# Seventh-products for the V columns, quarter products in the recurrence, and one block for experts and combination

## The reference

```python
# first block: attention with forget gates, then an MLP with squared ReLU
mod = silu(c) @ w_ada + b_ada                 # six vectors: shift, scale, gate, twice
h = rms_norm(x, norm_mix) * (1 + sc_m) + sh_m
qkv, f = h @ fox_w_in                         # 3 x 1024 columns, and 16 for the gates
x = x + g_m * (attention(norm(q), norm(k), v, cumsum(log_sigmoid(f))) @ fox_w_out)
x = x + g_f * (square(relu(h2 @ w_mlp_in)) @ w_mlp_out)

# second block: pooling and a recurrence per head (64 wide), then routed experts
z = x @ w_in ; zm = z + (z_prev - z) * mu     # z_prev: the token before
r, k, v = zm columns ; w, a, g from small two-step products
state = state * decay + sa * (kk * a) + v * k ; out = state . r   # token by token
y = (group_norm(out) + bonus) * g
h = layer_norm(alpha * x + [pool, y] @ w_out)
y = sum of 2 of 32 experts: (silu(h @ gate) * (h @ up)) @ down, weighted
out = layer_norm(alpha * h + y)
```

## Time and profile before

| what | value |
|---|---|
| median of three runs | 3013.24 us |
| profiled execution, its own time | 3023.13 us |
| its span | 3021.4 us |
| PE busy | 2836.5 us (94%), 18832 records |
| DVE busy | 1538.4 us (51%) |
| ACT busy | 725.1 us (24%) |
| POOL busy | 265.6 us (9%) |

### The profile page before, as it was taken

How to read it: one execution, slowest core, us unless ns; L and a number is a source line. 1 busy time by engine, 2 the same in 40 slices (tenths; PEclk the granted TensorE clock), 3 DMA queues, 4 the chain that set the end, 5 groups by cost and what they waited for, 6 DMA issues and landing times. The chain is left out here.

```text
span 3021.4 us, 48468 instructions
## 1 busy us (share of the span) xinstructions
PE 2836.5 (94%) x18832; PEld 1851.9 (61%) x18832; DVE 1538.4 (51%) x4129; ACT 725.1 (24%) x1635; POOL 265.6 (9%) x343
## 2 busy tenths in 40 slices
PE   4999989999999999999999999999999896999996
PEld 3886456664588544886444777777777554444442
DVE  5543056771355566655564666666666466111115
ACT  3211055551210000000002344444444200111111
POOL 0000011100000000000000122222222100010002
PEclk7999999999999999999999999999999897999998
DMA  5010033321022453224443100000000121999965
GB/s 224 29 47 38 0 105 99 108 83 42 14 84 84 167 181 139 84 86 162 161 177 144 57 25 26 2 26 16 12 25 2 50 87 43 351 358 352 355 242 195
DMA packets 103937, 338.62 MB, mean 112 GB/s; under 512 B 6944, under 2 KB 16672, under 8 KB 94640
## 3 DMA queue, kind: packets, MB, share of 16 engines
q1 hardware_dynamic: 96816, 310.55, 28.6%
q0 software_dynamic: 6912, 25.17, 2.3%
HBM read 302.60 MB, written 33.10 MB: 111 GB/s over the span
## 5 line engine op out<-in xcount | busy, mean ns | idle before, releaser
L1854 PE MATMUL mixing_ps<-all_main,pre_ws 128*128 128x256 f32 x1152 | 315.5, 397 | 0.0
L1189 PE MATMUL mlp_ps<-mlp_w2s,all_main 128*128 128x512 f32 x512 | 239.6, 592 | 0.0
L2790 PE MATMUL ex_pg<-all_main,ex_xT 128*128 128x512 f32 x512 | 226.9, 596 | 0.0
L1854 PEld LDWEIGHTS mixing_ps<-all_main,pre_ws 128*128 128x128 f32 x1152 | 200.0, 189 | 30.3
L1189 PE MATMUL mlp_ps<-all_main 128*128 128x512 f32 x384 | 183.2, 593 | 0.7 <-DVE all_main L1402 0.7
L2790 PEld LDWEIGHTS ex_pg<-all_main,ex_xT 128*128 128x128 f32 x512 | 98.0, 192 | 123.3 <-issue 123.3
L1189 PEld LDWEIGHTS mlp_ps<-mlp_w2s,all_main 128*128 128x128 f32 x512 | 96.6, 190 | 117.8 <-issue 104.6
L2180 POOL TENSOR_TENSOR all_tail<-all_tail,pre_cst 128x256 f32<-128x256 f32 x120 | 103.6, 878 | 430.5 <-DVE all_tail L2236 290.0
L1189 PEld LDWEIGHTS mlp_ps<-all_main 128*128 128x128 f32 x384 | 72.6, 190 | 93.4 <-issue 68.5
L2924 DVE TENSOR_TENSOR ex_hid<-ex_pg,ex_sil 128x256 f32<-128x256 f32 x32 | 13.6, 425 | 223.8 <-ACT ex_sil L2872 223.8
L1139 PE MATMUL mlp_ps<-all_main,all_early 128*128 128x256 f32 x512 | 121.0, 379 | 0.0
(11 more groups left out here) (440 smaller groups left out, 5039.8 us busy)
## 6 DMA issues: line engine op xcount, KB each, us to landing
mlp_w2s<-in_w SPq DMA_DIRECT2D x64, 1024.0 KB, 4.9
all_main<-in_w_gu SPq DMA_DIRECT2D x32, 2048.0 KB, 9.3
all_early<-in_w SPq DMA_DIRECT2D x32, 1024.0 KB, 4.9
att_wa<-in_w_ada SPq DMA_DIRECT2D x32, 512.0 KB, 3.7
all_early<-in_w_d SPq DMA_DIRECT2D x16, 1024.0 KB, 10.9
all_main<-in_w_d SPq DMA_DIRECT2D x16, 1024.0 KB, 11.2
y_rows<-ex_y SPq DMA_DIRECT2D x32, 512.0 KB, 3.0
qkv_wq<-in_w_qkv SPq DMA_DIRECT2D x6, 2048.0 KB, 7.7
```

What stands on the lines that cost most here:

```text
L1189: last = nc.tensor.matmul(ps[:, PRODUCTS.index(name), :], lhsT=lhsT, rhs=rhs, start=j == 0, stop=j == FPAIRS - 1)
L1854: last = nc.tensor.matmul(ps[:, bank, 0:UT], lhsT=ws[:, n, k, :], rhs=xT[:, k, (col + NB) % S:(col + NB) % S + UT], start=(k == 0), stop=( ...
L2790: last = nc.tensor.matmul(pg[:, n % 2, :], lhsT=xT[:, n % 2, k, :], rhs=gu[n][:, k, :], start=(k == 0), stop=(k == KT - 1))
```

## The change

Four edits are merged.

1. **Q, K, V**: all six chunks go by seven products. `S` and `T1`, `T2` move from the V columns of `main` to `xres`, and `stage_attention` loads x into `xres` again (two DMAs of 2 MB in SyncE's queue at p == 3). Squares and norms only for the first four chunks. `wf` and `fb` are loaded by `stage_start`, behind its own weights.
2. **Recurrence, quarter products**: the r and v projections (sixteen of 24 products a unit) are each four 64x64 matmuls in place of one of 128x128. The lower half of the contraction writes a second bank (4 for r, 1 for v), and VectorE adds that bank to ScalarE's copy of the first.
3. **Recurrence, order**: the gate product stands ahead of the keys, its copy behind the keys' copy; ScalarE copies level 2 out ahead of the square root and level 3 ahead of the normalisation; the transposes move from level 4 to level 5; r and v products are placed anew.
4. **Experts and combination** are one block, `stage_experts_combine`. The residual is scaled by alpha and the diagonal weights are made on VectorE at the head of the block; gain and bias rows are loaded there. GpSimd starts gathering as soon as the last rows are stored. VectorE adds product and residual with the sum for the mean, ScalarE squares with the mean taken off, VectorE scales.

```diff
@@ stage_qkv
-        S1, S2, S4 = ([main[:, 2 * n + k // 2, 2 * D + (k % 2) * NB:...] for k in range(HK)] for n in range(3))
+        S1, S2, S4 = ([sums[:, 2 * n + k // 2, (k % 2) * NB:(k % 2 + 1) * NB] for k in range(HK)] for n in range(3))
...
-                for c in range(SEVENTHS):
+                for c in range(CHUNKS):
...
-                pe.wait_ge(part, part_at(SEVENTHS - 1, 2, "c12"))
-                for c in range(SEVENTHS, CHUNKS):
...
@@ stage_attention, sync
+                    if p == 3:
+                        for half in range(2):
+                            sp.dma_start(xres[:, half * TT // 2:(half + 1) * TT // 2, :],
+                                         x[half * NB:(half + 1) * NB, :].rearrange("(t p) d -> p t d", p=P)).then_inc(x_back, 16)
@@ stage_rwkv
-        pe_a = Steps(s.sem("pe_make"), "wa k kk_sum r g v gram")
+        pe_a = Steps(s.sem("pe_make"), "wa g k kk_sum r v gram")
...
+                    def project_keys():
...
+                        for k in range(KT):
+                            last = nc.tensor.matmul(ps[:, B_BANK, 0:UT], lhsT=ws[:, 1, k, :], rhs=columns(k, slice(0, P)), ...)
...
+                        banks = (A_BANK, 4) if n == 0 else (B_BANK, 1)
...
                         for k in ks:
-                            last = nc.tensor.matmul(ps[:, bank, 0:UT], lhsT=ws[:, n, k, :], rhs=xT[:, k, ...],
-                                                    start=(k == 0), stop=(k == KT - 1))
+                            for half in range(2):
+                                for m in range(2):
+                                    last = nc.tensor.matmul(ps[heads(m), banks[half], 0:UT], lhsT=ws[heads(half), n, k, heads(m)],
+                                                            rhs=columns(k, heads(half)), start=(k == 0), stop=(k == KT - 1))
...
-                        project(1, range(0, 8), B_BANK)
+                        nc.tensor.matmul(ps[:, B_BANK, UT:2 * UT], lhsT=up[:, 2, :], rhs=lora_in[:, 1, bass.ds(col, UT)],
+                                         start=True, stop=True).then_inc(pe_a.sem, 1)
+                        project_keys()
...
@@ between(l), behind(l): products k of r (0) and v (2)
#  before: between 0: r0 | 1: r1-2 | 2: r4-5 | 3: r7 v0 | 4: turn, v2-3 | 5: gate, v5 ; behind 1: r3 | 2: r6 | 3: v1 | 4: v4 | end: v6-7
#  after:  between 0: r0-1 | 1: r2-3 | 2: r5-6 | 3: v0-1 | 4: v3-4 | 5: turn, v6 ; behind 1: r4 | 2: r7 | 3: v2 | 4: v5 | end: v7
...
+                            if l == TOP and nxt:
+                                wait(pe, dve_a, u, "r_z")
...
+                    if nxt:
+                        wait(pe, dve_a, u, "v_z")      # ahead of line 2042
@@ stage_rwkv, scalar
+                        copy(act_a, mixed(u), ps[:, 7, UT:2 * UT])
...
+                    x_out(2)
                     if prev:
                         wait(act, dve_y, y, "y_eps")
                         nc.scalar.activation(rstd[:, 1, :], rstd[:, 0, :], ACT.Sqrt).then_inc(act_y.sem, 1)
-                    x_out(2)
+                    x_out(3)
...
@@ stage_rwkv, vector
-                    make(None, tt, T0[:], Z[:, 0, 0:UT], Z[:, 0, 1:], ALU.subtract)
+                    make(None, tt, Z[:, 0, 1:], ps[:, 4, 0:UT], Z[:, 0, 1:], ALU.add)
+                    make("r_z", tt, T0[:], Z[:, 0, 0:UT], Z[:, 0, 1:], ALU.subtract)
...
+                    make(None, tt, Z[:, 2, 1:], ps[:, 1, 0:UT], Z[:, 2, 1:], ALU.add)
+                    make("v_z", tt, T0[:], Z[:, 2, 0:UT], Z[:, 2, 1:], ALU.subtract)
@@ stage_experts_combine
+                for n in range(2):
+                    pool.wait_ge(y_out[n], 16 * (EXPERTS // 2 + 1))
...
+                def weigh_rows(t):                      # 4 matmuls, no residual product
...
+                    nc.scalar.activation(xT[:, t % 2, :, :]..., hres[:, t, :], ACT.Square, bias=mv[:, t, 1:2],
+                                         accum_out=mv[:, t, 2:3]).then_inc(squared, 1)
...
+                for t in range(TT):                     # vector, at the head of the block
+                    nc.vector.tensor_scalar(hres[:, t, :], hres[:, t, :], ALPHA, None, ALU.mult).then_inc(scaled, 1)
...
+                    nc.vector.tensor_tensor_reduce(out=hres[:, t, :], in0=ps[...], in1=hres[:, t, :], op0=ALU.add, op1=ALU.add,
+                                                   accum_out=mv[:, t, 0:1]).then_inc(added, 1)
...
+                    nc.vector.scalar_tensor_tensor(out=y[:, t % 2, :], in0=hres[:, t, :], scalar=mv[:, t, 1:2], in1=rows[:, 0, :],
+                                                   op0=ALU.add, op1=ALU.mult).then_inc(shifted, 1)
```

338 lines of the change are left out of this document (145 added, 193 removed).

## The result

The kernel after took 2943.26 us in the median of four runs (2937.95 to 2943.34) against 3013.87 us before (four runs, 3011.2 to 3015.65): ratio 0.9762, 95% interval 0.9745 to 0.9779. Forecast were 2942 us and a range of 2922 to 2982.

What follows compares the result with a forecast made beforehand. TensorE's passes bound Q, K, V and part of the recurrence's half-levels, the dependent chain the others. 42 + 12.3 + 1.9 + 15.5 - 0.5 = 71.2 us saved gave 2952 us profiled, 2942 from the median; range 2922 to 2982.

Steps and rivals of the forecast that it cites:

- V chunks, 12.3 us: Q, K, V stage: two V chunks as seven products take 97.6 us instead of 109.9, gaining 12.3 us.
- Gate weights, 1.9 us: Kernel start: weights requested one block earlier shorten the first product's 3.30 us wait; 1.9 us taken, bounds 1 and 3.3.
- The recurrence, 42 us: Recurrence: quarter products and new order save net 1.84 us a unit over 23 units, less 0.5 for the first: 42 us.
- so it is covered, barely: Recurrence, before level 4's addition: VectorE's 0.42 us r addition fits in 1.28 us of idle time, so costs nothing.
- Rival 1: Recurrence: VectorE's additions and the later copies lie on the path, costing 19 us: 2961 us; chance 0.14.
- The 0.2 us a passage: Recurrence, TensorE: each switch between 64x64 and 128x128 drains about 0.2 us, gone when both neighbours are 64x64.
- rival 3: Recurrence: quarters sharing a row half run one after the other, a product taking 0.85 us: 108 us, 3050; chance 0.06.
- rival 4: Recurrence: each weight load waits for the running product, 0.27 us more a product, 68 us in all: 3010; chance 0.05.
- rivals 2: Recurrence: the 0.2 us stays at each burst, tiled or not; only 11 us gained there: 2973 us; chance 0.15.
- The last stage, 15.5 us: Experts and combination: earlier gather and start, VectorE pace 4.2 us a tile; gain 15.5 us, bounds 8 and 20.
- The experts' head: Start of the experts' block: residual scaling and diagonals on VectorE, up to 2.2 us bare, 0.5 us cost taken.
- rival 5: Recurrence: the granted clock falls, as to 1.2 GHz without projections; a falling clock or something unseen: chance 0.04.

Runs made afterwards that it cites:

- the second profile: The kernel before, run and profiled once more with no edit: 3015.99 us, profiled span 3014.2 us.
- the first profile: The original profiled execution of the kernel before, unchanged: 3023.13 us, of which the span is 3021.4 us.
- Experiment 3: Kernel after without VectorE's two second-bank additions, leaving out the lower 64 rows' contribution to r and v: 2935.23 us, ratio 0.974.
- experiment 4: Kernel after with VectorE's addition and transpose of level 4 moved ahead of the two operations that make r: 2939.11 us, ratio 0.9754.
- experiment 2: Kernel after with r and v products whole 128x128 again in the new order, without second bank or VectorE additions: 2965.92 us, ratio 0.9838.
- 8: Kernel after with level 2's sums of squares as eight 64x64 products into two banks instead of two 128x128 ones: 2933.55 us, ratio 0.9728.
- experiment 5: Kernel after with the four quarters of each r or v product issued so that row halves take turns: 2934.14 us, one run.
- Experiment 7: Kernel after with every engine skipping the empty spare-block loop as a whole, and gain and bias rows loaded behind the first expert weights: 2935.28 us, ratio 0.9736.
- the three edits together: Kernel after with level 4's addition moved ahead, sums of squares in quarters, and spare loop skipped with later gain and bias rows: 2924.58 us, ratio 0.9705.

## Why the prediction was right

The forecast of 2942 us met the median of 2943.26. The two large parts came as they were worked out. Some of the closeness is luck: inside a unit, misses of both signs cancel.

- **V chunks, 12.3 us.** Exact: 292.9 us for six chunks (69.5 to 362.4), 48.8 each, TensorE busy 291.3. From the first to the last product of the stage it is 292.4 or 292.5 in all ten profiles of the new kernels, 304.8 in both of before:

```profile
69.50:362.40 292.90, 291.30 (x1345) 254.95 (x1344) 124.91 (x265) 41.47 (x94) 3.78 (x2) 1.00 0.08 30
```

- **Gate weights, 1.9 us.** Met against the second profile; the start of the seventh-products lies between 68.9 and 70.2 us in the new kernels, so this is known to half a microsecond or so. Against the first profile the same place shows 5.5 us: there the gate product took 16.7 us instead of 13.9, with a granted clock of 0.82. Reading x again costs nothing that shows above the 3 us by which the attention stage differs from profile to profile.
- **The recurrence, 42 us.** 22 steady intervals gave 40.3 us (658.5 to 618.2), 1.83 a unit where the steps gave 1.84. The other 3.0 of the table's 43.3 are the last unit, 24.2 us here and 27 to 28 in seven of the other nine new kernels: luck, by the clock. By steps: levels 1 and 3 0.34 + 0.33 (forecast 0.35 each), level 2 0.66 (0.54), level 4 0.50 (0.52), level 5 0.21 (0.22), behind it 0.51 (0.37), chain-bound half-levels 0.03 to 0.05 each where nothing was forecast, against it 0.42 + 0.14 (0.43 + 0.08). So 0.39 us a unit came on top of what was counted (0.12 at level 2, 0.14 behind level 5, 0.13 in the chain-bound half-levels) and about as much was lost; that the sum is met to 0.01 is luck. One step was wrong in sign: "so it is covered, barely" of the r addition. The half-level behind level 4 grew by 0.29. The idle 1.28 us at 2054.15 was taken as room for one more operation, but the operations beside it did not keep their durations: the two behind the addition grew from 0.48 and 0.22 to 0.83 and 0.57. Experiment 3 gives the addition 0.22 of the 0.29, experiment 4 gets all of it back by order. Rival 1 was priced at both additions bare, 19 us. Without them 22 x 0.22 = 5 us go in the steady units and 3.8 at the start, so they cost about 9 us, near half of that price.
- **The mechanism.** The 0.2 us a passage goes when both neighbours are 64x64 (experiments 2 and 8), and quarters that share a row half don't wait for each other (5). Two quartered products take 0.98 us; rival 3 has 1.7 for them, rival 4 1.39. So rivals 2, 3 and 4 fall. The Trainium skill's statement (TensorEngine Tiling (Array Packing), Key Properties) that a change of the tiling mode drains TensorE agrees with experiments 2 and 8: 1.67 against 1.33 and 2.07 against 1.58 us, with a pause of 0.15 us ahead of the whole products in both. Its rule on weight loads and row groups (TensorE: Matmul & The Clock Gate, Part 3, The mechanism) is not borne out: in experiment 5 two of a product's eight loads change their neighbour's row half and the beat stays within 0.01 us, and in experiment 2, where every load takes all rows, loads of 0.19 us run beside the passes, which from the second on start 0.22 us apart.
- **The last stage, 15.5 us.** Measured 12.5 in the one profile of the kernel after, but 14.7 to 16.6 from the last copy to the end in the six kernels of the experiments with the same code there. The pace of 4.05 us a tile is the 4.2 forecast. TensorE's way through the loop over spare blocks was read from before as 13.3 us from the last copy, and those six kernels have 13.0 to 13.1: "It begins at 2963.3 instead of 2971.65" holds, and the 15.9 after are of that profile. Experiment 7 shows that this loop, and not the gather, holds TensorE: the rows are there 10.7 us after the copy. Another 0.4 went at the start, 6.3 us from TensorE's first product to VectorE's first pass against 5.9 (6.0 to 6.5 in the six). At the end, from VectorE's last pass to the end of the span, all profiles show either 3.1 us, as forecast, or, as after, 4.1.
- **The experts' head.** 0.5 us were forecast for VectorE's scaling; the delay is 1.0 and it is the transfer of gain and bias (512 KB each over all partitions) ahead of the first gather. The prediction named that transfer and gave it no price.
- **Not forecast: +1.8 us while the first unit is prepared.** With quarters the stretch from the last start of line 1584 to the first batch of line 2037 is 49.2 us, with whole products 47.0, before 47.4. The prediction had put this unit at 1.3 us less than before. The v addition stands bare there, TensorE idles 2.28 us instead of 1.78, and the granted clock falls to 0.50, that is to 1.2 GHz, in the rows that follow:

```profile
1648.00:1652.00 4.00, 2.06 (x34) 1.73 (x34) 2.51 (x11) 0.10 (x1) 0.00 (x0) 0.76 0.04 10
1652.00:1656.00 4.00, 4.00 (x16) 3.69 (x17) 3.24 (x9) 1.41 (x6) 2.52 (x3) 0.50 0.00 0
...
1648.00:1652.00 4.00, 2.60 (x13) 1.94 (x11) 3.64 (x10) 0.37 (x1) 0.97 (x1) 1.00 0.60 222
1652.00:1656.00 4.00, 3.62 (x50) 3.32 (x51) 3.25 (x13) 1.01 (x4) 1.24 (x2) 1.00 0.01 2
```

The first two rows are of the kernel after, the last two of the one with whole products, which stays at 1.00. Experiment 3 parts the causes: with quarters but without the additions TensorE idles 1.81 us, the clock stays at 1.00, and the stretch is 45.4 us. So it is the additions, and not the quarters, that let the clock fall. That is rival 5 of the prediction in one small place.

## What to carry to other kernels

Where a dependent chain of small tiled matmuls is filled with large ones, count the passages between the array's shapes: here each pair cost 0.3 to 0.35 us, nearly as much as a projection product (0.43), and cutting the filler into the chain's own shape at the same column count removed them, at the price of a second bank and an addition on another engine. Before placing that addition, look at what else runs beside it and put the chain's own operation first (0.32 us a unit for moving one line). When blocks are merged so that one engine can start early, look at what each of the others still has to step through: the gather was ready 2.4 us before TensorE had left an empty loop (5 in the profile of the kernel after). And before you explain a difference of 3 us in one stage of one profile, look at the same stage in the profiles of kernels that share its code.

## What the runs showed of the hardware

- Some of VectorE's operations get 0.35 us longer in one step where GpSimd runs beside them: 0.48 to 0.83 and 0.22 to 0.57 in the kernel after, at their old duration where GpSimd is idle (experiment 4). Others keep theirs: in each unit after, the subtraction at 2035.69 (0.43) and the transpose at 2034.90 (0.45) run beside GpSimd and are no longer than alone. What decides, no run shows. The runs moved the operations in time; none took GpSimd's away, so its part is read from the order of time. The Trainium skill (GPSIMD Engine Reference, 1. Specifications) has the two engines share their way to the buffers for some of VectorE's operations; the rows agree that some such meetings cost, and add the step of 0.35 us.
- The last unit of the recurrence, which has no projections, takes 22.3 us where the granted clock stays at 1.00 (experiment 5), 24.2 where it falls late (after, and with whole products) and 27.0 to 28.0 where it falls early (all others, the three edits together among them); before it took 27.7 and 27.2. With the first products of a stage (125.7 or 122.8 us for line 1095's 256) this makes differences of 3 to 4 us each in the span of single executions whose steady parts agree to 0.1%.
